# Squares of the last norm shared by ScalarE and VectorE, VectorE's tiles ahead of the last sums, another PSUM bank for v's first product, biases loaded earlier

## The chip, the cores and the metric

One core of one Trainium2 chip runs the whole kernel. The metric is the device time of one execution in microseconds (us); lower is better. The engines are TensorE (PE, with its weight load PEld), VectorE (DVE), ScalarE (ACT), GpSimd (POOL) and SyncE (SP), which here only issues transfers. All of them work in order, each from its own stream, and meet through semaphores.

## The reference

A decoder layer over 1024 tokens of width 1024, all float32, and a last RMSNorm:

```python
h = rmsnorm(x, norm1_g)
q, k, v, u = split(h @ w_in)                    # 4 x 512 columns
attn = diff_attention(q, k, v, ...)             # 4 heads, causal, two softmaxes each
pool = multiscale_pool(u, ...)                  # trailing means, windows 2, 4, 8, 16
x = x + concat(attn, pool) @ w_out
h = rmsnorm(x, norm2_g)
# top 4 of 32 experts; each expert, on its rows:
gate = minimum(xb @ w_gate[e] + b_gate[e], 7)
up   = clip(xb @ w_up[e] + b_up[e], -7, 7)
y    = (gate * sigmoid(1.702 * gate) * (up + 1)) @ w_down[e] + b_down[e]
x = x + sum over a token's experts of its gate value * y
out = rmsnorm(x, final_g)                       # x / sqrt(mean(x*x) + eps) * g
```

## The kernel before, in words

Tokens lie on the 128 partitions in 8 tiles of 128 rows (TB = 8), or transposed with features on the partitions. The work goes through five stages.

1. Input norm and projections. A list `jobs` sets the order of PE's products; each job is one PSUM bank of 512 columns that DVE or ACT empties. `bank_of(n)` gives the bank: n modulo 8 for the jobs up to `first_late` (34 jobs, so the last k product, job 33, sits in bank 1), and after them banks 1 and 3 in turn, beginning with v's first product (L294). A product waits until the bank's previous user has been emptied (`user_before`, `emptied`). After v's first product come the first attention scores, which wait until the first 34 jobs have been emptied.
2. Attention and pooling, 32 units of a token tile and a head, with the v and u products mixed in by hand (`slots_a`).
3. Output product, second norm and routing, tile by tile (b = 0 to 7). SP stores x1 and h2 of each tile to HBM (L399, L401). Before the last tile's stores it waits for the whole output product and loads the three bias tables of 32 rows (L397). PE turns them (`turn_bias`, L1677) behind the last logits, and ACT copies them out (L814). The tables lie in hT, ACT's square of the last tile goes to the scratch tile `junk_h`.
4. 32 experts, one after another. Each is six groups of 64 matmuls on 2 MB of weights that SP loads ahead; POOL gathers the tokens' rows and adds results back into HBM (`x_rows`).
5. The last norm, laid around the last group of products of expert 31. When the rows of the experts before it are in HBM, SP loads x1's eight tiles into `x2` (L439). POOL gathers expert 31's own rows (L622). ACT squares and sums each tile (`squares_of_rows`, L857). POOL multiplies tiles 0 to 3 by g (`tensor_tensor`, L640), each behind its tile's square. DVE waits for all eight sums (`squares_f`), computes 1/sqrt of the means in 12 small steps (`rsqrt_mean_dve`, L87 to L100) and signals `rstd_f`. Then ACT scales tiles 0 to 3 (L863), and DVE does tiles 4 to 7 in one step each (`normed_row`, L1363). SP writes the tiles out in the order 4, 1, 5, 2, 6, 3, 7 (L443, L446), POOL writes tile 0 (L643). DVE also adds the bias to the two halves of expert 31's last product: `down(0)` ahead of the wait for the sums, `down(1)` between its tiles 6 and 7 (both L1254 here). PE turns these halves back (L1873). `last_rows` adds them to the gathered rows (L1350), ACT squares (L873), DVE takes the second rsqrt and scales (L1359), and POOL scatters these rows over the output (L632). Before this scatter POOL waits until every one of the eight tiles has been written.

The order on DVE at the end of expert 31 is this:

```python
down(0)
f.n = 0
f.did(dve.memset(ss_l, 1.0))
dve.wait_ge(gf_in, 16)
dve.wait_ge(squares_f, TB)
rsqrt_mean_dve(dve, f, rstd[:, :], ss[:, :], tmp[:, :, :], D)
f.need()
dve.sem_inc(rstd_f, 1)
for b in range(SCALED, TB - 1):     # SCALED = 4
    normed_row(b)
down(1)
last_rows(nh)                       # begins with normed_row(TB - 1)
```

Of the kernel before, what the change touches and what calls it, by code (L numbers as in the profile page):

```python
# [12 lines left out]
P = 128  # L13
S, D = 1024, 1024
TB, KC = S // P, D // P
# [5 lines left out]
E, TOPK = 32, 4  # L21
# [13 lines left out]
SCALED = 4  # L35
# [67 lines left out]
def layer(nc, d, rows, out):  # L103
    with ExitStack() as ctx:
        sb = lambda name, shape, dt=F32: ctx.enter_context(nc.sbuf_tensor(name, shape, dt))
        sem = lambda name: ctx.enter_context(nc.semaphore(name))
        ps = ctx.enter_context(nc.psum_tensor("ps", [P, 8, HALF], F32))


        x = sb("x", [P, TB, D])  # L110
        xn = sb("xn", [P, TB, D])
        hT = sb("hT", [P, KC, S])
# [8 lines left out]
        ident = sb("ident", [P, P])  # L121
# [6 lines left out]
        bias = early[:, :].rearrange("p (i m e) -> p i m e", i=3, e=E)  # L128
# [4 lines left out]
        lam = sb("lam", [P, 8])  # L133
        ss, rstd, tmp = sb("ss", [P, TB]), sb("rstd", [P, TB]), sb("tmp", [P, 3, TB])
# [24 lines left out]
        x1T = xn[:, 1].rearrange("p (k t) -> p k t", t=P)  # L159
        h2 = [hT[:, 6], hT[:, 7], xn[:, 2], xn[:, 3]]  # L160

        junk_h, ss_h = xn[:, 4], lam[:, 6:7]
        late = xn[:, 6:8].rearrange("p a n -> p (a n)")
        r = Routes()
        r.slot = late[:, 0:256].rearrange("p (b e) -> p b e", e=E)
# [17 lines left out]
        flat = hT[:, :, :].rearrange("p k n -> p (k n)")  # L183
        taken = [0]

        def of_hT(*shape, dt=F32):

            n = math.prod(shape)
            words = n if dt in (F32, I32) else n // 2
            a = flat[:, taken[0]:taken[0] + words]  # L190
            taken[0] += words
            assert taken[0] <= KC * S
            names = "abc"[:len(shape)]
            a = a if dt == F32 else a.bitcast(dt)
            if len(shape) == 1:
                return a
            return a.rearrange(f"p ({' '.join(names)}) -> p {' '.join(names)}", **{c: s for c, s in zip(names, shape)})

        xg = of_hT(2, D)
        xT, aT = of_hT(KC, SLOTS), of_hT(KC, SLOTS)  # L200

        bias_rows = flat[0:E, 2 * D:2 * D + 3 * D].rearrange("p (i n) -> p i n", i=3)
        gt, ut, sg = (of_hT(4, SLOTS) for _ in range(3))
        tok = of_hT(TB, 6, dt=BF16)
        tab = [of_hT(4, dt=I32) for _ in range(3)]
# [16 lines left out]

        x2 = qk[:, :, :, :].rearrange("p a (b c) n -> p (a b) (c n)", c=2)

        junk_f, x_last = x[:, 7], xg
        small_f = x[:, 4, MORE * E:MORE * E + 10]
        ss_l, rstd_l, tmp_l = small_f[:, 0:2], small_f[:, 2:4], small_f[:, 4:10].rearrange("p (i h) -> p i h", h=2)

        x_in = [sem(f"x_in{b}") for b in range(TB)]
        vec_in, lam_ld, g2_in, wp_in, rw_in, rb_in = (sem(n) for n in ("vec_in", "lam_ld", "g2_in", "wp_in", "rw_in", "rb_in"))  # L230
        w_in, w_q_in = [sem(f"w_in{i}") for i in range(6)], sem("w_q_in")
        biases_in = sem("biases_in")
# [11 lines left out]
        out_mm, x1_ready, h2_ready, sq2 = (sem(n) for n in ("out_mm", "x1_ready", "h2_ready", "sq2"))  # L244
# [22 lines left out]
        squares_f, ready_f, ready_a, rstd_f, times_g = (sem(n) for n in ("squares_f", "ready_f", "ready_a", "rstd_f", "times_g"))  # L267
# [8 lines left out]
        first_late = len(jobs)  # L276
# [13 lines left out]
        def bank_of(n):  # L290

            if n == len(jobs) - 1:
                return 6
            return n % 8 if n < first_late else (1, 3)[(n - first_late) % 2]  # L294

        def user_before(n):

            return next((m for m in range(n - 1, -1, -1) if bank_of(m) == bank_of(n)), None)
# [46 lines left out]
        with nc.Block() as block:  # L345

            @block.sync
            def _(sp):
# [42 lines left out]
                sp.wait_ge(o_done, TB)  # L391
                sp.dma_start(w[2], weights(0, 2)).then_inc(w_ready[2], 16)
                for b in range(TB):
                    if b == TB - 1:
                        sp.wait_ge(out_mm, 2 * TB)
                        for i, bias in enumerate((d["b_gate"], d["b_up"], d["b_down"])):
                            sp.dma_start(bias_rows[:, i, :], bias[0]).then_inc(biases_in, 16)  # L397
                    sp.wait_ge(x1_ready, 2 * (b + 1))
                    sp.dma_start(rows.x1[b * P:(b + 1) * P, :], x[:, b, :]).then_inc(x1_st[b], 16)  # L399
                    sp.wait_ge(h2_ready, b + 1)  # L400
                    sp.dma_start(rows.h2[b * P:(b + 1) * P, :], h2[b % 4]).then_inc(h2_st[b], 16)  # L401
# [10 lines left out]
                for e in range(E):  # L412
                    for g, (src, c) in enumerate(sources):
                        n = e * GROUPS + g
# [261 lines left out]
            def _(act):  # L676
# [173 lines left out]
                        turn_in(j + 1)  # L850

                def squares_of_rows(again):
                    for b in range(TB):
                        act.wait_ge(x_in[b], 32 + 16 * again)
                        if b or again:
                            act.wait_ge(squares_f, again * TB + b)
                        act.activation(junk_f, x2[:, b, :], ACT.Square, accum_out=ss[:, b:b + 1]).then_inc(squares_f, 1)  # L857

                squares_of_rows(0)
                act.wait_ge(rstd_f, 1)  # L860
                for b in range(SCALED):
                    act.wait_ge(times_g, b + 1)
                    act.activation(x2[:, b, :], x2[:, b, :], ACT.Copy, scale=rstd[:, b:b + 1]).then_inc(ready_a, 1)  # L863
                act.wait_ge(squares_f, TB)
                act.sem_inc(passed, 1)

                def squares_of_last(nh):
# [23 lines left out]
            def _(dve):  # L891
# [441 lines left out]
                f = Order(dve, order_f)  # L1333

                def last_rows(nh):

                    normed_row(TB - 1)
                    dve.wait_ge(last_in, 32)
                    last_tab = tab[(E - 1) % 3]
                    for h in range(nh):  # L1340
                        n = HALVES[h]
                        by = last_tab[0:n, 2 + h:3 + h].bitcast(F32)
                        if nh == 1:
                            dve.wait_ge(pair_free, PAIRS + E * GROUPS)
                            dve.scalar_tensor_tensor(y[:, 0, :], t_rows, by, x_last[:, 0, :], ALU.mult, ALU.add).then_inc(last_z, 1)
                        else:
                            dve.wait_ge(back_mm[h], E + 1)
                            halves = lambda a: a.rearrange("p (a n) -> p a n", a=2)
                            at = (side, 0)[h]
                            dve.scalar_tensor_tensor(halves(y[0:n, h, :]), ps[0:n, at:at + 2, :], by, halves(x_last[0:n, h, :]),  # L1350
                                                     ALU.mult, ALU.add).then_inc(last_z, 1)
                    dve.wait_ge(last_sq, nh)
                    g = Order(dve, order_f, f.n)
                    rsqrt_mean_dve(dve, g, rstd_l, ss_l, tmp_l, D)
                    g.need()
                    assert g.n == STEPS_L
                    for h in range(nh):
                        n = HALVES[h]
                        dve.scalar_tensor_tensor(x_last[0:n, h, :], y[0:n, h, :], rstd_l[0:n, h:h + 1], g2[0:n, :], ALU.mult,  # L1359
                                                 ALU.mult).then_inc(last_f, 1)  # L1360

                def normed_row(b):
                    dve.scalar_tensor_tensor(x2[:, b, :], x2[:, b, :], rstd[:, b:b + 1], g2[:, :], ALU.mult, ALU.mult).then_inc(ready_f, 1)  # L1363
# [3 lines left out]
                def item(nh):  # L1367
                    n = (P, SLOTS)[nh - 1]
                    down = (lambda c: rows_down(E - 1, c)) if nh == 1 else (lambda c: down_in(E - 1, n, c))
                    for c in range(2):  # L1370
                        gate_in(E - 1, n, c)
                        up_in(E - 1, n, c)
                    down(0)
                    f.n = 0
                    f.did(dve.memset(ss_l, 1.0))
                    dve.wait_ge(gf_in, 16)
                    dve.wait_ge(squares_f, TB)
                    rsqrt_mean_dve(dve, f, rstd[:, :], ss[:, :], tmp[:, :, :], D)
                    f.need()
                    dve.sem_inc(rstd_f, 1)  # L1380
                    for b in range(SCALED, TB - 1):
                        normed_row(b)
                    down(1)
                    last_rows(nh)
                past_first(dve, wide, item)

                def all_rows():
                    dve.wait_ge(squares_f, 2 * TB)
                    g = Order(dve, order_f, f.n + STEPS_L)
                    rsqrt_mean_dve(dve, g, rstd[:, :], ss[:, :], tmp[:, :, :], D)  # L1390
                    g.need()
                    for b in range(TB):
                        normed_row(b)
# [41 lines left out]
            def _(pe):  # L1435
# [42 lines left out]
                for t in range(TB // 2):  # L1478
                    pe.wait_ge(x_in[t], 16)
                    for k in range(KC - 1):  # L1480
                        ins = pe.transpose(ps[:, bank_of(k), t * P:(t + 1) * P], x[:, t, k * P:(k + 1) * P], ident[:, :])
# [192 lines left out]
                def turn_bias(i, at):  # L1674
                    pe.wait_ge(biases_in, 48)
                    for m in range(KC):
                        ins = pe.transpose(ps[:, at, m * E:(m + 1) * E], bias_rows[:, i, m * P:(m + 1) * P], ident[0:E, 0:E])  # L1677
                    ins.then_inc(bias_mm, 1)

                turn_bias(0, 4)  # L1680
# [186 lines left out]
                with pe.If(width_of(pe, E - 1) > 0):  # L1867
                    pe.wait_ge(y_ready, 2 * E)
                    for c in range(2):
                        pe.wait_ge(pair_free, E * GROUPS + PAIRS - 1 + c)  # L1870
                        for h, n in enumerate(HALVES):
                            for k in range(4 * c, 4 * c + 4):
                                ins = pe.transpose(ps[0:n, (side, 0)[h] + c, (k - 4 * c) * P:(k - 4 * c + 1) * P],  # L1873
                                                   yT[:, k, h * P:h * P + n], ident[:, :])
# [35 lines left out]
def build(nc, d, out):  # L1910
    layer(nc, d, Rows(nc), out)
# [21 lines left out]
```

## Time and profile before

| | us |
|---|---|
| median of 3 runs (2072.66 to 2073.78) | 2072.96 |
| the profiled execution, its own time | 2074.92 |
| its span, first to last instruction | 2073.2 |
| PE busy | 2011.8 (97% of the span) |
| DVE, ACT, POOL busy | 655.5, 283.8, 232.9 |

The mean granted TensorE clock was 0.99 of full speed. The rows further down are of the profiled execution; their times count from its first instruction. A row of the timeline gives start, duration, engine, line and operation, and in brackets how long the engine had been idle before it and what released it. Rows whose engine ends in q (SPq) are the issue of a transfer, not its movement.

### The profile page before, as it was taken

Reading aid. Unit: us, or ns where it says so; the run is one execution under the profiler, and the core shown is the slowest. Engines: PE = TensorE matmul, PEld = TensorE weight load, DVE = VectorE, ACT = ScalarE, POOL = GpSimd, SP = SyncE. Lnnn points to the kernel's source line nnn. Section 1 sums busy time; section 2 is a strip of 40 time slices with the busy share of each in tenths; the row PEclk is TensorE's granted clock in tenths of the full one; section 3 lists DMA queues with packets and bytes.
Section 4 is the critical chain, followed back from the end, with each engine's and each line's share of the span. In section 5 each row is a group of like instructions: output and inputs, shape, how many; then the busy total and the mean of one; then the engine's idle time right before and its main releaser. Section 6 shows DMA issues by size and latency. Waiting matters only on the chain.

```text
span 2073.2 us, 32125 instructions
## 1 busy us (share of the span) xinstructions
PE 2011.8 (97%) x13457; PEld 1643.8 (79%) x13458; DVE 655.5 (32%) x1363; ACT 283.8 (14%) x457; POOL 232.9 (11%) x381
## 2 busy tenths in 40 slices
PE   8999988996999999999999999999999999999996
PEld 4444455554998898889788999988888888989996
DVE  3115676443223222222222332222222222222223
ACT  2001245111011001101001010111010100100103
POOL 0001333212000001000001010010000000000103
PEclk9999999997999999999999999999999999999998
DMA  4210022214878879998999988899899998887855
GB/s 173 81 41 1 1 92 84 100 61 152 305 248 305 307 272 322 321 329 296 321 322 318 309 294 272 286 319 335 312 304 322 319 319 310 279 299 260 287 189 199
DMA packets 231449, 500.89 MB, mean 242 GB/s; under 512 B 7766, under 2 KB 8303, under 8 KB 231298
## 3 DMA queue, kind: packets, MB, share of 16 engines
q1 hardware_dynamic: 218880, 454.46, 61.0%
q0 software_dynamic: 12368, 44.26, 8.6%
q8 instruction: 113, 1.85, 0.4%
q14 instruction: 38, 0.31, 0.0%
q10 hardware_dynamic: 50, 0.01, 0.0%
HBM read 463.63 MB, written 35.13 MB: 241 GB/s over the span
## 4 chain that ended last, share of the span: by engine, by line
PE 72%; DMA 1%; DVE 1%; issue 1%; SPq 0%; ACT 0%; POOL 0%; POOLq 0%; DVEq 0%; ACTq 0%
PE ps L1694 57%; PE ps L1721 12%; PE ps L1708 2%; PE ps L1714 1%; PE ps L1701 1%; DMA qk<-x_rows 1%; DMA out<-qk 0%; DVE x L1254 0%; DMA hT<-h_rows,hT 0%; DMA x_rows<-x,hT 0%; DVE qk L1363 0%; SPq L439 0%; DVE xn L1221 0%; ACT hT L821 0%; ACT x L857 0%
## 5 line engine op out<-in xcount | busy, mean ns | idle before, releaser
L1694 PE MATMUL ps<-hT,qk 128*128 128x128 f32 (+8 forms) x4096 | 501.7, 284 | 6.8 <-issue 6.8
L1694 PEld LDWEIGHTS ps<-hT,qk 128*128 128x128 f32 x4096 | 493.5, 192 | 16.6 <-issue 16.0
L1721 PE MATMUL ps<-w_ring,hT 128*128 128x512 f32 x576 | 251.8, 593 | 0.0
L1694 PE MATMUL ps<-hT,u_all 128*128 128x128 f32 (+8 forms) x2048 | 247.7, 282 | 0.0
L1694 PE MATMUL ps<-hT,v 128*128 128x128 f32 (+8 forms) x2048 | 247.7, 282 | 0.0
L1694 PEld LDWEIGHTS ps<-hT,v 128*128 128x128 f32 x2048 | 244.6, 191 | 0.0
L1694 PEld LDWEIGHTS ps<-hT,u_all 128*128 128x128 f32 x2048 | 244.6, 191 | 0.0
L1694 PE MATMUL ps<-hT,w_ring 128*128 128x132 f32 (+7 forms) x1792 | 233.8, 291 | 5.0 <-DVE x L1254 3.6
L1694 PEld LDWEIGHTS ps<-hT,w_ring 128*128 128x128 f32 x1792 | 229.3, 190 | 7.4 <-issue 7.0
L1721 PEld LDWEIGHTS ps<-w_ring,hT 128*128 128x128 f32 x576 | 107.5, 190 | 126.7 <-issue 126.3
L558 POOL DMA_INDIRECT hT<-h_rows,hT x46 | 45.3, 986 | 1148.9 <-issue 672.1
L825 ACT ACTIVATE hT<-hT 128x768 f32<-128x768 f32 x64 | 53.9, 842 | 855.5 <-DVE hT L1235 855.5
L1467 PE MATMUL ps<-hT,w_ring 128*128 128x512 f32 x384 | 168.9, 595 | 1.3 <-DMA w_ring<-in_w_in 1.3
L1467 PEld LDWEIGHTS ps<-hT,w_ring 128*128 128x128 f32 x384 | 71.5, 190 | 86.7 <-issue 83.7
L1241 DVE TENSOR_TENSOR hT<-ps,early 128x512 f32<-128x512 f32 (+1 forms) x64 | 51.7, 808 | 241.3 <-PE ps L1694 234.0
L1232 DVE TENSOR_TENSOR hT<-ps,early 128x512 f32<-128x512 f32 (+1 forms) x64 | 51.7, 808 | 212.9 <-PE ps L1694 191.1
L563 POOL DMA_INDIRECT x_rows<-x,hT x44 | 70.1, 1593 | 266.9 <-ACT x L836 220.1
L821 ACT COPY hT<-ps 128x1024 f32<-128x1024 f32 x64 | 51.2, 800 | 338.8 <-PE ps L1708 298.5
L1262 DVE TENSOR_TENSOR x<-ps,x 128x512 f32<-128x512 f32 x36 | 24.9, 692 | 220.4 <-PE ps L1721 220.4
L1254 DVE TENSOR_TENSOR x<-ps,early 128x768 f32<-128x768 f32 x28 | 26.8, 958 | 193.5 <-PE ps L1694 193.5
L1239 DVE TENSOR_TENSOR hT<-hT 128x512 f32<-128x512 f32 (+1 forms) x64 | 52.4, 818 | 65.8 <-ACT hT L825 65.8
L1203 DVE COPY hT<-ps 128x12 f32<-128x12 f32 x31 | 5.3, 171 | 180.5 <-PE ps L1701 180.5
(250 smaller groups left out, 1470.6 us busy)
## 6 DMA issues: line engine op xcount, KB each, us to landing
w_ring<-in_w_down SPq DMA_DIRECT2D x64, 2048.0 KB, 7.9
qk<-in_w_gate SPq DMA_DIRECT2D x32, 2048.0 KB
qk<-in_w_up SPq DMA_DIRECT2D x32, 2048.0 KB
v<-in_w_gate SPq DMA_DIRECT2D x32, 2048.0 KB, 10.5
u_all<-in_w_up SPq DMA_DIRECT2D x32, 2048.0 KB, 8.7
x<-in_b_down SPq DMA_DIRECT2D x32, 512.0 KB, 11.6
w_ring<-in_w_in SPq DMA_DIRECT2D x3, 2048.0 KB, 9.0
x<-in_x SPq DMA_DIRECT2D x8, 512.0 KB, 12.4
```

The costliest lines, as they stand in the source:

```text
L558: return pool.indirect_dma_start(out=xg[0:n, h, :], out_offset=None, in_=rows.h2[:, :], in_offset=bass.IndirectOffsetOnAxis(ap=tab_e[0:n, ...
L563: return pool.indirect_dma_start(out=rows.x1[:, :], out_offset=bass.IndirectOffsetOnAxis(ap=tab_e[0:n, h:h + 1].bitcast(U32), axis=0), in_ ...
L821: act.copy(xT[:, :, h * P:h * P + n], turned_in[h]).then_inc(xT_ready, 1)
L825: act.activation(sg[:, :, :], gt[:, :, :], ACT.Sigmoid, scale=ALPHA).then_inc(sg_ready, 1)
L1232: dve.tensor_tensor(gt[:, :, 0:n], pair[2 * c % PAIRS][:, :, 0:n], bcast(r.bias[:, 0, 4 * c:4 * c + 4, e], n), ALU.add).then_inc(pair_free, 1)
L1239: dve.tensor_tensor(sg[:, :, 0:n], gt[:, :, 0:n], sg[:, :, 0:n], ALU.mult).then_inc(gate_s, 1)
L1241: dve.tensor_tensor(ut[:, :, 0:n], pair[(2 * c + 1) % PAIRS][:, :, 0:n], bcast(r.bias[:, 1, 4 * c:4 * c + 4, e], n), ALU.add).then_inc(pai ...
L1254: dve.tensor_tensor(yT[:, 4 * c:4 * c + 4, 0:n], pair[(4 + c) % PAIRS][:, :, 0:n], bcast(r.bias[:, 2, 4 * c:4 * c + 4, e], n), ALU.add).th ...
L1467: ins = pe.matmul(bank, ring[:, tile_of[what] % 2, k, a * P:(a + 1) * P], hT[:, k, b * HALF:(b + 1) * HALF], start=k == 0, stop=k == KC - 1)
L1694: ins = pe.matmul(bank[:, m, 0:n], w[g][:, k, m * P:(m + 1) * P], rhs[:, k, 0:n], start=k == 0, stop=k == KC - 1)
L1708: ins = pe.transpose(turned_in[h][:, k, :], xg[0:n, h, k * P:(k + 1) * P], ident[0:n, 0:n])
L1721: ins = pe.matmul(ps[:, 2 * (g % PAIRS), :], aT[:, k, 0:P], w[g][:, k, :], start=k == 0, stop=k == KC - 1)
```

## The change

- `bank_of`: the late jobs take banks 3 and 1 in turn, so that v's first product goes to bank 3. The last user of that bank is job 27.
- The biases are loaded at b = 5 of SP's loop, with no wait for the output product. They go to other places (`xn[0:E, 5]`, `hT[0:E, 4]`, `xn[0:E, 4]`), and `junk_h` moves from `xn[:, 4]` to `xn[:, 0]`.
- ACT squares tiles 0 to 3 of the last norm alone. DVE squares tiles 4 to 7 with `tensor_tensor_reduce`, the instruction that it uses for squares of the first norm (L897), into another scratch tile. Its wait on `squares_f` is for four.
- `down(0)` moves from ahead of the squares to behind the rsqrt; tile 7 moves ahead of `down(1)`, so that DVE's four tiles follow one another.

```diff
-            return n % 8 if n < first_late else (1, 3)[(n - first_late) % 2]
+            return n % 8 if n < first_late else (3, 1)[(n - first_late) % 2]
...
-                    if b == TB - 1:
-                        sp.wait_ge(out_mm, 2 * TB)
+                    if b == TB // 2 + 1:
                         for i, bias in enumerate((d["b_gate"], d["b_up"], d["b_down"])):
-                            sp.dma_start(bias_rows[:, i, :], bias[0]).then_inc(biases_in, 16)
+                            sp.dma_start(bias_rows[i], bias[0]).then_inc(biases_in, 16)
...
-                    for b in range(TB):
+                    for b in range(TB if again else TB // 2):
                         act.wait_ge(x_in[b], 32 + 16 * again)
...
                         act.activation(junk_f, x2[:, b, :], ACT.Square, accum_out=ss[:, b:b + 1]).then_inc(squares_f, 1)
...
-                    normed_row(TB - 1)
                     dve.wait_ge(last_in, 32)
...
-                    down(0)
                     f.n = 0
                     f.did(dve.memset(ss_l, 1.0))
+                    for b in range(TB // 2, TB):
+                        dve.wait_ge(x_in[b], 32)
+                        f.need()
+                        f.did(dve.tensor_tensor_reduce(junk_v, x2[:, b, :], x2[:, b, :], 1.0, 0.0, ALU.mult, ALU.add,
+                                                       accum_out=ss[:, b:b + 1]))
                     dve.wait_ge(gf_in, 16)
-                    dve.wait_ge(squares_f, TB)
+                    dve.wait_ge(squares_f, TB // 2)
                     rsqrt_mean_dve(dve, f, rstd[:, :], ss[:, :], tmp[:, :, :], D)
                     f.need()
                     dve.sem_inc(rstd_f, 1)
-                    for b in range(SCALED, TB - 1):
+                    down(0)
+                    for b in range(SCALED, TB):
                         normed_row(b)
                     down(1)
                     last_rows(nh)
```

## Rows read from the trace of the kernel before

**Rows 1.** The page's chain that ended last: shares of the span by line.

```profile
PE ps L1694 57%; PE ps L1721 12%; PE ps L1708 2%; PE ps L1714 1%; PE ps L1701 1%; DMA qk<-x_rows 1%; DMA out<-qk 0%; DVE x L1254 0%; DMA hT<-h_rows,hT 0%; DMA x_rows<-x,hT 0%; DVE qk L1363 0%; SPq L439 0%; DVE xn L1221 0%; ACT hT L821 0%; ACT x L857 0%
```

**Rows 2.** Busy time by stretch: PE, PEld, DVE, ACT, POOL; PEclk, DMA share, GB/s.

```profile
522.00:1990.00 1468.00, 1462.11 (x11147) 1316.71 (x11146) 400.05 (x720) 149.32 (x167) 110.37 (x86) 1.00 0.88 303
...
2053.00:2054.00 1.00, 1.00 (x9) 1.00 (x8) 1.00 (x2) 1.00 (x2) 0.59 (x1) 1.00 0.44 180
2054.00:2064.00 10.00, 2.51 (x20) 1.98 (x18) 8.35 (x18) 3.94 (x6) 0.81 (x1) 0.78 1.02 396
```

**Rows 3.** Timeline at v's first product.

```profile
127.61 7.11 PE L1461 MATMUL ps<-w_ring,hT 128*128 128x512 f32 x16 [0.88 <-DVE qk L934]
```

**Rows 4.** Timeline between the output product and the first expert.

```profile
487.87 0.34 SPq L397 DMA_DIRECT2D hT<-in_b_gate  x1
...
491.42 1.18 PE L1677 MATMUL ps<-ident,hT 32*128 32x32 f32 x16 [0.39 <-DMA hT<-in_b_down]
...
492.64 0.34 SPq L401 DMA_DIRECT2D h_rows<-xn  x1
...
493.50 0.21 PE L1630 MATMUL ps<-member,tri 128*128 128x32 bf16 x1 [0.90 <-DVE member L1118]
```

**Rows 5.** Timeline of the last norm.

```profile
2039.25 9.31 POOL L640 TENSOR_TENSOR qk<-qk,g 128x1024 f32<-128x1024 f32 x4
...
2041.12 1.06 ACT L857 ACTIVATE x<-qk 128x1024 f32<-128x1024 f32 x1
...
2043.20 1.06 ACT L857 ACTIVATE x<-qk 128x1024 f32<-128x1024 f32 x1 [0.93 <-DMA qk<-x_rows]
...
2046.54 1.06 ACT L857 ACTIVATE x<-qk 128x1024 f32<-128x1024 f32 x1 [2.19 <-DMA qk<-x_rows]
...
2047.78 1.06 ACT L857 ACTIVATE x<-qk 128x1024 f32<-128x1024 f32 x1
...
2049.02 0.17 DVE L87 TENSOR_SCALAR tmp<-ss 128x8 f32<-128x8 f32 x1 [3.20 <-ACT x L857]
...
2051.37 4.27 ACT L863 ACTIVATE qk<-qk,rstd 128x1024 f32<-128x1024 f32 x4 [2.44 <-DVEq L1380]
2051.44 3.68 DVE L1363 SCALAR_TENSOR_TENSOR qk<-qk,rstd,g 128x1024 f32<-128x1024 f32 x3 [0.16 <-DVE rstd L100]
2052.75 0.34 SPq L446 DMA_DIRECT2D out<-qk  x1
...
2055.03 0.95 DVE L1254 TENSOR_TENSOR x<-ps,early 128x768 f32<-128x768 f32 x1
...
2055.21 1.94 PE L1873 MATMUL ps<-ident,x 128*128 128x128 f32 x16 [0.64 <-issue]
...
2057.09 2.46 DVE L1350 SCALAR_TENSOR_TENSOR x<-ps,hT 128x1024 f32<-128x1024 f32 x2
...
2063.06 2.47 DVE L1359 SCALAR_TENSOR_TENSOR hT<-x,g 128x1024 f32<-128x1024 f32 x2
2067.62 0.99 POOL L632 DMA_INDIRECT out<-hT  x1 [12.80 <-issue]
```

**Rows 6.** The chain in order of time, the last wait ahead of POOL's scatters.

```profile
2058.76 7.57 DMA out<-qk
```

**Rows 7.** Timeline in the attention stage where POOL and DVE instructions meet.

```profile
176.70 1.03 POOL L502 TENSOR_TENSOR xn<-xn 128x512 f32<-128x512 f32 x1 [116.30 <-DVE xn L1029]
...
176.90 0.85 DVE L1015 SCALAR_TENSOR_TENSOR soft<-soft,lam 128x1 f32<-128x1 f32 x1
...
214.71 1.22 DVE L983 TENSOR_TENSOR v<-u_all 128x1023 f32<-128x1023 f32 x1
...
214.87 1.95 POOL L502 TENSOR_TENSOR xn<-xn 128x512 f32<-128x512 f32 x1 [27.15 <-DVE xn L1029]
...
216.02 1.88 DVE L983 TENSOR_TENSOR v<-v 128x1022 f32<-128x1022 f32 x1
```

**Rows 8.** All squares of the first norm on DVE: shortest, median and longest, ns.

```profile
L897 DVE CUSTOM_DVE_ANT_0 u_all<-x x4: 1225/1226/1227, 5.9 to 20.0; 128x1024 f32<-128x1024 f32 x4
```

More of the change, by code:

```diff
@@ L160, in layer @@
         h2 = [hT[:, 6], hT[:, 7], xn[:, 2], xn[:, 3]]
-        junk_h, ss_h = xn[:, 4], lam[:, 6:7]
+        junk_h, ss_h = xn[:, 0], lam[:, 6:7]
         late = xn[:, 6:8].rearrange("p a n -> p (a n)")
@@ L200, in layer @@
         xT, aT = of_hT(KC, SLOTS), of_hT(KC, SLOTS)
-        bias_rows = flat[0:E, 2 * D:2 * D + 3 * D].rearrange("p (i n) -> p i n", i=3)
+        bias_rows = [xn[0:E, 5], hT[0:E, 4], xn[0:E, 4]]
         gt, ut, sg = (of_hT(4, SLOTS) for _ in range(3))
@@ L223, in layer @@
         x2 = qk[:, :, :, :].rearrange("p a (b c) n -> p (a b) (c n)", c=2)
-        junk_f, x_last = x[:, 7], xg
+        junk_f, junk_v, x_last = x[:, 7], xn[:, 3], xg
         small_f = x[:, 4, MORE * E:MORE * E + 10]
@@ L852, in squares_of_rows @@
                 def squares_of_rows(again):
-                    for b in range(TB):
+                    for b in range(TB if again else TB // 2):
                         act.wait_ge(x_in[b], 32 + 16 * again)
                         if b or again:
-                            act.wait_ge(squares_f, again * TB + b)
+                            act.wait_ge(squares_f, again * (TB // 2) + b)
                         act.activation(junk_f, x2[:, b, :], ACT.Square, accum_out=ss[:, b:b + 1]).then_inc(squares_f, 1)
@@ L863, in _ @@
                     act.activation(x2[:, b, :], x2[:, b, :], ACT.Copy, scale=rstd[:, b:b + 1]).then_inc(ready_a, 1)
-                act.wait_ge(squares_f, TB)
+                act.wait_ge(squares_f, TB // 2)
                 act.sem_inc(passed, 1)
@@ L1387, in all_rows @@
                 def all_rows():
-                    dve.wait_ge(squares_f, 2 * TB)
+                    dve.wait_ge(squares_f, TB // 2 + TB)
                     g = Order(dve, order_f, f.n + STEPS_L)
@@ L1676, in turn_bias @@
                     for m in range(KC):
-                        ins = pe.transpose(ps[:, at, m * E:(m + 1) * E], bias_rows[:, i, m * P:(m + 1) * P], ident[0:E, 0:E])
+                        ins = pe.transpose(ps[:, at, m * E:(m + 1) * E], bias_rows[i][:, m * P:(m + 1) * P], ident[0:E, 0:E])
                     ins.then_inc(bias_mm, 1)
```

## The prediction

> **What bounds the kernel now.** I read the chain that ended last first. By line it is PE's products of the experts, the matmuls of L1694 and L1721 [rows 1]; the view by stretch says the same, since from 522 to 1990 us PE works 1462.1 of 1468 us at a granted clock of 1.00 [rows 2]. The change takes no work from PE. So only two kinds of place can move the time: a gap in PE's stream ahead of the experts, which moves everything after it, and the stretch behind the last products, where PE no longer matters.
>
> Second I read the timeline at the edges. There is one gap that the change touches, 0.88 us ahead of v's first product, released by a DVE eviction [rows 3].
>
> Third, the end. In the last norm ACT squares tile 6 at 2046.54, when it lands, and tile 7 at 2047.78; DVE's rsqrt starts at 2049.02, its first tile at 2051.44, the first output write is issued at 2052.75 [rows 5]. From then on the transfers are the limit: 180 GB/s in the microsecond from 2053, 396 GB/s at a share of 1.02 over the next ten [rows 2]. The last write is issued at 2058.76 and lands 7.57 us later, at 2066.33 [rows 6]; POOL's first scatter goes at 2067.62 [rows 5], and the span ends at 2073.2, 6.9 us after the landing. So the end follows the moment at which output writes begin, not the moment at which the last tile is ready. The other strand, the last expert's own rows, is ready at 2063.06 + 2.47 = 2065.53 and waits for the writes [rows 5].
>
> **Bank of v's first product.** In bank 1 it waits for the eviction of the last k product. In bank 3 the previous user is six jobs older, so the wait is gone. v's first product takes 7.11 us of PE [rows 3], far more than the eviction, so the scores behind it, which want that eviction too, find it done. What follows hangs on PE or on waits counted from it, the transfers of later weights included, so the gain is passed on whole: -0.88 us. Its bounds are 0, if another wait takes it up further on, and -0.88.
>
> **Biases.** Three loads leave SP's queue at 487.87 and go to an idle moment at b = 5. PE waited 0.39 us for them at 491.42, but behind the two turns it waits again, 0.90 us, for DVE's `member` at 493.50 [rows 4]. What comes earlier in PE only lengthens that second wait. The x1 store of tile 7 gets up to 1.3 us earlier, yet h2's store, which the gather needs as well, waits for the norm and stays at 492.64 [rows 4]. At b = 5 SP has nothing queued. Cost 0; without the second wait it would be a gain of 0.39.
>
> **Squares on two engines.** Counted without anything in between, nothing is won: the last sum is not late for want of an engine but because tile 6 lands at 2046.54. DVE has both late tiles, 6 and 7, one after the other, and one square takes it 1.226 us [rows 8]. From 2046.54 that is 2046.54 + 2 x 1.23 = 2049.0, and the rsqrt starts at 2049.02 today.
>
> Something is in between, though. POOL multiplies tiles 0 to 3 from 2039.25 for 9.31 us, 2.33 each [rows 5], and today DVE has nearly nothing to do then. In the attention stage the two meet. POOL's 128x512 multiply takes 1.03 us alone; begun 0.16 us behind a DVE tensor_tensor it takes 1.95, until 216.82. The next DVE one begins at 216.02 and takes 1.88 in place of 1.22: it ends 1.08 us after POOL's end. Even a 128x1 instruction begun 0.20 us after POOL's start takes 0.85 and ends 0.02 after it [rows 7]. So they take turns by whole instructions: one of DVE with two inputs in SBUF does not run beside one of POOL. The squares read `x2` twice and are of that kind. No row shows a square itself against POOL, so the bounds are no hold at all and a hold for every one.
>
> The Trainium skill (GPSIMD Engine Reference, Specifications) says that GpSimd's SBUF interfaces are shared with VectorE, with contention from VectorE instructions that have two SBUF inputs; it gives no price. By it the squares are held and the time is the 2076.9 below; by the row of the squares alone, which ran with POOL idle, it would be 2073.0.
>
> I take the hold. Tile 4 is there by about 2041.1 (ACT took it at 2041.12 with no wait), inside POOL's first multiply, 2039.25 to 2041.58. Then they alternate: square 4 to 2042.66, multiply 1 to 2044.96, square 5 (landed 2043.2) to 2046.04, multiply 2 to 2048.35, square 6 to 2049.43, multiply 3 to 2051.75, square 7 to 2052.8. As a sum: 2039.25 + 9.31 + 4 x 1.08 = 2052.88. The rsqrt starts some 0.05 later, at 2052.9, not at 2049.02: **+3.9 us**. If every turn costs a full 1.23 it is +4.5. POOL's multiplies end 3.2 us later, at 2051.75. ACT needs the fourth three scalings of 1.07 after its start, which itself moves to 2055.3 [rows 5], so that costs nothing.
>
> **down(0) behind the rsqrt.** It takes 0.95 us, as the same instruction at 2055.03 [rows 5], and now stands between rstd and DVE's first tile. SP's order begins with that tile, and the write of tile 1 is behind it in SP's queue. So the first write moves by another **+0.9** to 2052.75 + 3.9 + 0.9 = 2057.6. The first half was hidden in DVE's wait for the squares; that cover is gone. Tile 1's write then follows at once (0.84 us behind today's first), which may give back 0.1; I keep +0.9 within 0.5 to 1.0.
>
> **Tile 7 ahead of down(1).** The four tiles at 1.23 end at about 2061.2 and down(1) at 2062.2, against 2055.98 today: +6.2. Its followers are PE's turns, L1350, ACT's squares, the second rsqrt and L1359. If PE's part keeps its 1.1 us, L1359 starts at 2069.3; PE has been idle long by then, and at the half clock that the mean of 0.78 contains [rows 2] it is 2.2 us and 2070.4. Its two results come at 2071.6 and 2072.9. The writes land at 2066.33 + 4.8 = 2071.1, POOL wants the first result about half a microsecond later, and the second 1.3 us after the first. It fits, with hardly anything to spare. Cost 0.
>
> **Sum.** -0.88 + 0 + 3.9 + 0.9 = +3.9 us. On the profiled execution that is 2074.92 + 3.9 = 2078.8 (span 2077.1). This execution lies 1.96 above the median of the runs, so the median is 2072.96 + 3.9 = **2076.9**.
>
> **The rivals.**
> - No hold: the squares do not share what the multiplies need. For it: they are another instruction than those in rows 7. Against it: they read two streams from SBUF at 1.226 us, as the tensor_tensor with its 1.22 does. Then +0.9 for down(0) against -0.88: 2073.0.
> - The last rows become the gate, the slower side. PE's turns behind down(1) run at half clock and, with the first half's eight delayed into them, take 3.9 us (twice 1.94) in place of 1.1. L1359 then starts at 2072.1, its first result comes at 2073.3, POOL waits 1.7 us for it: 2078.6. It decides from about 0.1 us of delay beyond what I count.
> - The gap ahead of v only moves: something else in the attention stage takes the 0.88 us. PE is busy there with gaps of its own, which speaks a little for it. 2077.8.
> - Fewer turns: the last tiles' landings are set by one slow stretch of the load (2.19 us of waiting for tile 6), and if tile 4 came before POOL starts, square 7 would stand ahead of the last multiply. That takes 2.3 off: 2074.6.
>
> **How the numbers follow.** Turns with the writes as gate: 0.60, own range 2076.0 to 2077.8. No hold 0.13, last rows 0.12, gap moved 0.08, fewer turns 0.07. For this kernel 0.2%, 4.1 us, is about what a measurement can tell from no change, so slower begins at 2077.1. Above it lie the last rows (0.12), most of the moved gap (0.07) and a third of the likeliest case (0.21), that is 0.40. Faster would need 4.1 us, and nothing here has more than 0.9: 0.01. Same: 0.59. The range takes in no hold below and the last rows above: 2072.6 to 2078.8.
>
> **What the profile after would show.** v's first product with no idle time ahead. DVE rows of squares among the tail's rows, of some 1.5 to 3 us in place of 1.23, and POOL's four multiplies 3 us longer in total. L87 some 3.9 us later against the last landing, then L1254 ahead of four tiles, and the first output write 4.8 later. PE's turns of the biases without a wait, but the one for `member` longer. I am wrong if the squares show 1.23 us each beside POOL, or if POOL's scatter is released by L1359 and not by the last write.

## The result, and the profile after

The changed kernel takes 2078.07 us (median of 12 runs, 2076.20 to 2079.71), the kernel before, timed beside it, 2073.62 (12 runs, 2072.06 to 2074.74). The ratio is 1.0024, with a 95% interval of 1.0016 to 1.0031: 4.45 us slower, where +3.9 was forecast. The time lies in the stated range of 2072.6 to 2078.8, and 1.17 us above the forecast of 2076.9. 0.66 of that is the kernel before, whose median was 2072.96 when I forecast and is 2073.62 here; the other 0.5 is the change itself. It is also 0.3 above the range of the likeliest case (2076.0 to 2077.8). With 0.24% it is just beyond the 0.2% that separates slower from no change in the prediction, the side to which I had given 0.40, and "same" 0.59.

The timeline of the last norm in the changed kernel, the counterpart of [rows 5]:

```profile
2034.48 17.32 PE L1698 MATMUL ps<-hT,w_ring 128*128 128x180 f32 x112 [0.36 <-DVE hT L1247]
...
2036.46 9.28 POOL L639 TENSOR_TENSOR qk<-qk,g 128x1024 f32<-128x1024 f32 x4
...
2038.22 8.62 DVE L1377 CUSTOM_DVE_ANT_0 xn<-qk 128x1024 f32<-128x1024 f32 x1 [3.88 <-DMA qk<-x_rows]
...
2046.99 1.22 DVE L1377 CUSTOM_DVE_ANT_0 xn<-qk 128x1024 f32<-128x1024 f32 x1
...
2048.36 1.23 DVE L1377 CUSTOM_DVE_ANT_0 xn<-qk 128x1024 f32<-128x1024 f32 x1
...
2049.74 1.22 DVE L1377 CUSTOM_DVE_ANT_0 xn<-qk 128x1024 f32<-128x1024 f32 x1
...
2051.11 0.17 DVE L87 TENSOR_SCALAR tmp<-ss 128x8 f32<-128x8 f32 x1
...
2053.58 0.96 DVE L1254 TENSOR_TENSOR x<-ps,early 128x768 f32<-128x768 f32 x1 [0.21 <-DVE rstd L100]
2054.45 4.86 DVE L1362 SCALAR_TENSOR_TENSOR qk<-qk,rstd,g 128x1024 f32<-128x1024 f32 x4
...
2055.76 0.34 SPq L445 DMA_DIRECT2D out<-qk  x1
...
2060.24 1.97 PE L1877 MATMUL ps<-ident,x 128*128 128x128 f32 x8 [4.49 <-DVE x L1254]
...
2067.44 2.47 DVE L1358 SCALAR_TENSOR_TENSOR hT<-x,g 128x1024 f32<-128x1024 f32 x2
2070.74 0.99 POOL L631 DMA_INDIRECT out<-hT  x1 [14.12 <-DVE hT L1358]
```

POOL begins its multiplies at 2036.46 and ends them at 2045.74, as fast as before. DVE's square of tile 4 is released by its landing at 2038.22 and lasts 8.62 us, until 2046.84, which is 1.10 us behind POOL's end. The other three then take 1.22 or 1.23 each. The rsqrt starts 14.65 us after POOL's first multiply (2051.11 - 2036.46), where it was 9.77 in [rows 5] (2049.02 - 2039.25). Then comes down(0), 0.96 us, and then the first tile.

Two executions don't reach this stretch at the same moment, so I measure from the start of PE's last 112 matmuls. In the kernel before these start at 2037.26:

```profile
2037.26 17.32 PE L1694 MATMUL ps<-hT,w_ring 128*128 128x180 f32 x112 [0.36 <-DVE hT L1247]
```

There the first output write comes 15.49 us after it (2052.75) and the end 35.94 (2073.2); in the changed kernel 21.28 (2055.76 - 2034.48) and 41.82 (2076.3 - 2034.48). The tail is 5.9 us longer, and 5.8 of it is there when the writes begin.

The chain in order of time says that the writes are still what the end waits for, as in [rows 6]. It runs to the landing of the last write, 2061.29 + 8.16 = 2069.45:

```profile
2038.22 8.62 DVE xn L1377
...
2061.29 8.16 DMA out<-qk
```

The timeline puts L1358 as the releaser beside POOL's scatter (2070.74), the sign by which the prediction would have been wrong. It isn't so: L1358's first result, the only one that the first scatter needs, was there at about 2068.7. The scatter starts 1.29 us after the landing, and before it was 1.29 as well (2066.33 to 2067.62).

The view by stretch, the counterpart of [rows 2], shows the writes at nearly the same rate, 401 GB/s where it was 396. PE turns the second half of the last expert's rows at a granted clock of 0.50, which is its level of 1.2 GHz, after 4.49 us without work:

```profile
2057.00:2067.00 10.00, 1.97 (x8) 1.41 (x8) 7.17 (x15) 3.02 (x5) 0.00 (x0) 0.50 1.02 401
```

At v's first product, the counterpart of [rows 3], the idle time is gone:

```profile
125.58 7.03 PE L1465 MATMUL ps<-w_ring,hT 128*128 128x512 f32 x16
```

It starts 2.03 us earlier than in the execution of before. 0.88 of that is the gap; the other 1.15 is a difference between the two executions ahead of this place. By the start of the last 112 matmuls the lead is 2.78 us, and so these two spans differ by only 3.1 us (5.9 - 2.8). The medians differ by 4.45: over many executions the lead is smaller, 1.4 us if the tail is 5.9 us longer in all of them. 0.88 of that is the gap, the rest is not explained.

Around the biases, the counterpart of [rows 4]:

```profile
442.36 0.89 SPq L396 DMA_DIRECT2D xn<-in_b_gate  x1
...
490.47 0.32 SPq L400 DMA_DIRECT2D h_rows<-xn  x1
```

```profile
488.80 0.68 PE L1681 MATMUL ps<-ident,xn 32*128 32x32 f32 x8
489.32 1.01 PE L1681 MATMUL ps<-ident,hT 32*128 32x32 f32 x8
491.33 0.21 PE L1634 MATMUL ps<-member,tri 128*128 128x32 bf16 x1 [1.00 <-DVE member L1118]
```

The turns have no wait ahead of them any more. They take 1.53 us from first start to end (490.33 - 488.80) where they took 1.18, and the wait for `member` has grown from 0.90 to 1.00 us.

### The profile page after: what moved, and what is told of

Read it like the earlier page. It is cut to its first block, busy times and chain, and to the rows that moved or that the text cites. A ratio compares the mean times of both kernels' runs of the same rounds, so it can differ in the third digit from the quotient of the medians.

```text
span 2076.3 us, 32125 instructions
## 1 busy us (share of the span) xinstructions
PE 2012.2 (97%) x13457; PEld 1644.4 (79%) x13458; DVE 667.5 (32%) x1371; ACT 278.9 (13%) x449; POOL 232.2 (11%) x381
## 4 chain that ended last, share of the span: by engine, by line
PE 72%; DVE 1%; DMA 1%; issue 1%; SPq 0%; ACT 0%; POOL 0%; POOLq 0%; DVEq 0%
PE ps L1698 57%; PE ps L1725 12%; PE ps L1712 2%; PE ps L1718 1%; PE ps L1705 1%; DVE xn L1377 1%; DMA out<-qk 0%; DMA qk<-x_rows 0%; DVE x L1254 0%; DMA hT<-h_rows,hT 0%; DVE qk L1362 0%; DMA x_rows<-x,hT 0%; DVE xn L1221 0%; SPq L438 0%; ACT hT L820 0%
```

## The experiments

The tail is always the time from the start of PE's last 112 matmuls to the end of the span, in the profiled execution. Each tail is a single one. The kernel before, v_and_biases and v_bank_alone have the same last norm and show 35.9, 35.5 and 35.4 us, so I read nothing into differences of half a microsecond.

| kernel | median us (runs) | before beside it | ratio (95%) | first write, us into the tail | tail us |
|---|---|---|---|---|---|
| before | | | | 15.49 | 35.9 |
| changed | 2078.07 (12) | 2073.62 | 1.0024 (1.0016 to 1.0031) | 21.28 | 41.8 |
| squares_on_act | 2073.49 (11) | 2073.29 | 0.9999 (0.9990 to 1.0008) | 16.57 | 37.1 |
| down0_first | 2077.14 (11) | 2073.29 | 1.0018 (1.0009 to 1.0027) | 20.39 | 41.0 |
| v_and_biases | 2072.10 (11) | 2073.29 | 0.9995 (0.9986 to 1.0004) | 15.15 | 35.5 |
| pool_waits_own | 2077.15 (10) | 2073.29 | 1.0019 (1.0009 to 1.0028) | 20.11 | 40.7 |
| gather_late | 2070.11 (11) | 2072.90 | 0.9986 (0.9977 to 0.9995) | 13.42 | 33.9 |
| v_bank_alone | 2072.32 (11) | 2072.90 | 0.9997 (0.9988 to 1.0006) | 15.04 | 35.4 |
| no_multiplies | 2072.86 (1) | 2072.90 | | 15.93 | 36.7 |
| plain_product | 2077.15 (1) | 2072.90 | | 21.11 | 41.7 |

**squares_on_act: the squares back on ACT, the new order kept.**

```diff
-                    for b in range(TB if again else TB // 2):
+                    for b in range(TB):
...
-                    for b in range(TB // 2, TB):
-                        dve.wait_ge(x_in[b], 32)
-                        f.need()
-                        f.did(dve.tensor_tensor_reduce(...))
...
-                    dve.wait_ge(squares_f, TB // 2)
+                    dve.wait_ge(squares_f, TB)
```

> The changed kernel with all eight squares back on ACT; down(0) stays behind the rsqrt and tile 7 ahead of down(1). Measure of the tail: from the start of PE's last 112 matmuls to the end of the span, 35.9 us before and 41.8 us in the changed kernel. If DVE's squares beside POOL's multiplies are what costs most (theory), the tail is 36.9 us, the 0.95 us of down(0) above before, and the whole time is that of before within 0.5 us (0.9 gained at v, 0.95 lost here). If instead the order of down(0), the tiles and down(1) is what costs (rival: the last rows become the gate), the tail stays above 39 us and the time at 2 us or more over before.

The tail is 37.1 us and the time that of before. The timeline:

```profile
2044.59 1.06 ACT L857 ACTIVATE x<-qk 128x1024 f32<-128x1024 f32 x1
2048.18 4.27 ACT L863 ACTIVATE qk<-qk,rstd 128x1024 f32<-128x1024 f32 x4 [2.44 <-DVEq L1378]
2048.30 0.96 DVE L1254 TENSOR_TENSOR x<-ps,early 128x768 f32<-128x768 f32 x1 [0.21 <-DVE rstd L100]
...
2050.48 0.34 SPq L445 DMA_DIRECT2D out<-qk  x1
```

ACT's own square of tile 7 starts at 2044.59, and it is scaling tile 0 3.59 us later, as in [rows 5] (2051.37 - 2047.78). The squares on DVE cost 41.8 - 37.1 = 4.7 us by the tails. The medians against the kernel before beside each give 4.3 (4.45 - 0.20). The new order alone costs 37.1 - 35.9 = 1.2, in which down(0) is 0.96. The late down(1) shows only as the small rest, if at all.

**down0_first: down(0) ahead of the squares.**

```diff
+                    down(0)
                     f.n = 0
                     f.did(dve.memset(ss_l, 1.0))
...
                     dve.sem_inc(rstd_f, 1)
-                    down(0)
```

> The changed kernel with down(0) back ahead of the squares, where DVE waits anyway for POOL's multiplies to end. Theory: POOL's four multiplies run to their end whatever DVE does, the squares follow, so down(0) is hidden: first output write 0.9 us earlier against the start of PE's last matmuls, tail 40.9 us in place of 41.8, time about 3.6 us over before in place of 4.5. Rival (DVE's squares would be let in between if they came at other moments): tile 4's square starts only after down(0), so the order of the two engines changes and the tail moves by more than 1.5 us either way.

```profile
2035.51 9.31 POOL L639 TENSOR_TENSOR qk<-qk,g 128x1024 f32<-128x1024 f32 x4
...
2041.11 0.96 DVE L1254 TENSOR_TENSOR x<-ps,early 128x768 f32<-128x768 f32 x1 [7.74 <-PE ps L1698]
...
2042.23 3.67 DVE L1378 CUSTOM_DVE_ANT_0 xn<-qk 128x1024 f32<-128x1024 f32 x1 [0.16 <-DVE x L1374]
```

down(0), one of whose inputs is in PSUM, runs in 0.96 us beside POOL. The square, begun at 2042.23, waits again for POOL's end at 2044.82 and is done at 2045.90, 1.08 behind it. So asking 1.8 us or 6.7 us after POOL's start makes no difference to when the squares are done. The first write comes 0.9 us earlier and the tail is 0.8 shorter. The chain in order of time goes through the last rows here, in place of a write's landing:

```profile
2066.78 1.28 DVE hT L1358
...
2068.97 0.45 POOL out L631
```

That can't be what released the scatter. It is the second result of L1358, done at 2068.06, and the first scatter (`wait_ge(last_f, h + 1)`, h = 0) needs only the first, which was there at about 2066.8. The last output write, asked for by itself:

```profile
L445 SPq DMA_DIRECT2D out<-qk x1: 1248/1248/1248, 2059.4 to 2059.4; - x1
...
DMA to landing us min/median/max: 8.3/8.3/8.3
```

It lands at about 2067.7 (2059.38 + 8.3), and the scatter starts 1.3 us later, the same distance as in the kernel before and in the changed kernel. So the writes are the gate here too; the second result only happened to come at a step of POOL's way to its scatter.

**pool_waits_own: each multiply of POOL waits for the one before it.**

```diff
                         pool.wait_ge(squares_f, b + 1)
+                        if b:
+                            pool.wait_ge(times_g, b)
                         pool.tensor_tensor(x2[:, b, :], x2[:, b, :], g2[:, :], ALU.mult).then_inc(times_g, 1)
```

> The changed kernel with one added wait: each of POOL's four multiplies waits for the one before it to be finished. Theory (POOL keeps what both engines need as long as its next multiply is ready to go, and DVE gets in when POOL has to wait for its own result): DVE's squares come in between, tile 4's square takes some 1.5 to 3.5 us in place of 8.6, POOL's four multiplies stretch from 9.3 to 12 us or more, and DVE's rsqrt starts 13.6 us after POOL's first multiply, where it is 14.65 in the changed kernel: time about 1 us less. Rival (this kind of DVE instruction always loses against POOL): tile 4's square again lasts until POOL's last multiply ends, and nothing moves.

```profile
2038.39 2.37 POOL L641 TENSOR_TENSOR qk<-qk,g 128x1024 f32<-128x1024 f32 x1
...
2040.46 1.39 DVE L1379 CUSTOM_DVE_ANT_0 xn<-qk 128x1024 f32<-128x1024 f32 x1 [4.20 <-DMA qk<-x_rows]
2040.91 9.73 POOL L641 TENSOR_TENSOR qk<-qk,g 128x1024 f32<-128x1024 f32 x3
2042.87 2.27 DVE L1379 CUSTOM_DVE_ANT_0 xn<-qk 128x1024 f32<-128x1024 f32 x1 [1.01 <-DMA qk<-x_rows]
...
2046.00 2.43 DVE L1379 CUSTOM_DVE_ANT_0 xn<-qk 128x1024 f32<-128x1024 f32 x1 [0.85 <-DMA qk<-x_rows]
...
2048.58 3.14 DVE L1379 CUSTOM_DVE_ANT_0 xn<-qk 128x1024 f32<-128x1024 f32 x1
...
2051.86 0.17 DVE L87 TENSOR_SCALAR tmp<-ss 128x8 f32<-128x8 f32 x1
```

This is the picture of the prediction. The engines take turns; POOL's four multiplies last from 2038.39 to 2050.64, 12.3 us; the rsqrt starts 13.47 us after the first of them, where the prediction had 13.65 (2052.9 - 2039.25) and the changed kernel 14.65. A wait that seems idle makes the tail 1.1 us shorter; the medians (+3.9 us here, +4.45 in the changed kernel) agree in direction, but their intervals overlap. In these two kernels what decides is whether POOL has its next instruction ready.

**plain_product: DVE without the sum.** The sums of tiles 4 to 7 are left out.

```diff
-                        f.did(dve.tensor_tensor_reduce(junk_v, x2[:, b, :], x2[:, b, :], 1.0, 0.0, ALU.mult, ALU.add,
-                                                       accum_out=ss[:, b:b + 1]))
+                        f.did(dve.tensor_tensor(junk_v, x2[:, b, :], x2[:, b, :], ALU.mult))
```

> The changed kernel with a plain tensor_tensor product in place of the square with a sum on DVE (the sums of tiles 4 to 7 are left out). Theory (what matters is POOL's run of multiplies without a wait between them): tile 4's product also lasts until POOL's last multiply ends, some 8.6 us. Rival (the instruction with a sum is the one that cannot get in): tile 4's product takes under 4 us and POOL's multiplies are stretched beyond 9.3 us.

The four products of DVE by line, shortest, median and longest in ns:

```profile
L1377 DVE TENSOR_TENSOR xn<-qk x4: 1224/1225/8360, 2037.7 to 2048.9; 128x1024 f32<-128x1024 f32 x4
```

The longest takes 8.36 us: a plain tensor_tensor, of the kind that took turns with POOL in [rows 7], is shut out as well. So it is not a matter of the instruction with a sum.

**no_multiplies: POOL's four multiplies taken out.** Tiles 0 to 3 go out without the factor g.

```diff
-                        pool.tensor_tensor(x2[:, b, :], x2[:, b, :], g2[:, :], ALU.mult).then_inc(times_g, 1)
+                        pool.sem_inc(times_g, 1)
```

> The changed kernel without POOL's four multiplies by g (tiles 0 to 3 go out without the factor; the signal to ACT is kept). Theory: with POOL out of the way DVE squares each tile when it lands, 1.23 us each, and its rsqrt starts about 2.5 to 3.0 us after tile 6's landing, as ACT's did, not 7.8 us as in the changed kernel; tail of about 37 us in place of 41.8. Rival (the square on DVE is slow by itself in this place, or held by the transfers into x2): tile 4's square stays at several us.

```profile
2037.94 1.23 DVE L1377 CUSTOM_DVE_ANT_0 xn<-qk 128x1024 f32<-128x1024 f32 x1 [3.71 <-DMA qk<-x_rows]
...
2042.61 1.22 DVE L1377 CUSTOM_DVE_ANT_0 xn<-qk 128x1024 f32<-128x1024 f32 x1 [1.87 <-DMA qk<-x_rows]
...
2044.27 1.22 DVE L1377 CUSTOM_DVE_ANT_0 xn<-qk 128x1024 f32<-128x1024 f32 x1 [0.42 <-DMA qk<-x_rows]
...
2045.64 0.17 DVE L87 TENSOR_SCALAR tmp<-ss 128x8 f32<-128x8 f32 x1
```

With POOL quiet each square takes its 1.23 us when its tile lands, and the tail is 36.7 us. Yet the last square starts when tile 7 lands, and the rsqrt 1.37 us after that; ACT had 1.24 in [rows 5]. With the load as it is, shared squares win nothing even without the collision.

**v_and_biases and v_bank_alone: the last norm untouched.** The first is the kernel before with the new bank and the early biases (their parts of the diff, nothing else), the second with the new bank alone.

> The kernel before with the other bank for v's first product and the early biases, the last norm untouched. Theory: 0.9 us faster than before, all of it from the bank; no idle time ahead of L1461's first matmul (0.88 before) and the tail 35.9 us. Rival (the gap only moves): same time as before, and PE idle 0.88 us more elsewhere between v's first product and the experts.

> The kernel before with v's first product in bank 3 and nothing else. Theory: 0.9 us faster than before and the same as with the biases too (the biases are worth nothing). Rival (the early biases carry part of it): within 0.3 us of before, and slower than v_and_biases.

The idle time ahead of v's first product is gone in both. The medians lie 1.2 and 0.6 us below before, but both intervals hold 1, and the two kernels can't be told from each other. A gain of 0.9 us fits both, no gain is not excluded by the times, and how the 0.9 splits on the bank and the biases they don't say. For that I have only the profile.

The rival in which the gap only moves would make the stretch from v's first product to the start of the last 112 matmuls 0.88 us longer: 1909.65 us in the kernel before (2037.26 - 127.61), so 1910.5. In the nine profiled executions with the new bank it is 1907.1 to 1910.0 us (v_bank_alone: 2033.92 - 126.03 = 1907.89). That speaks against the rival. It does not settle it, as these nine differ by 3 us and there is one execution of before.

**gather_late: a version that beats both.** v_and_biases with one move: POOL gathers the last expert's rows behind its multiplies.

```diff
-                past_first(pool, wide[E - 1], rows_of_last)
...
                         pool.tensor_tensor(x2[:, b, :], x2[:, b, :], g2[:, :], ALU.mult).then_inc(times_g, 1)
+                    past_first(pool, wide[E - 1], rows_of_last)
```

> The kernel before with the other bank, the early biases and one more move: POOL gathers the last expert's own rows behind its four multiplies in place of ahead of them. The last norm's order is that of the kernel before, with all squares on ACT. Theory: x1's eight tiles are loaded without the gather's 0.77 MB beside them and the last tile lands 2 to 3 us earlier against the load's issue (16.2 us from the first issue to the start of tile 7's square before), DVE's rsqrt and the first output write follow, so the time is 2 to 3 us below v_and_biases. Rival: the slow pieces of the load are not the gather's doing, and the last square starts when it did: same time as v_and_biases within 0.5 us.

```profile
2029.41 5.08 SPq L438 DMA_DIRECT2D qk<-x_rows  x8
...
2035.57 9.33 POOL L638 TENSOR_TENSOR qk<-qk,g 128x1024 f32<-128x1024 f32 x4 [9.66 <-ACT x L856]
...
2043.21 1.06 ACT L856 ACTIVATE x<-qk 128x1024 f32<-128x1024 f32 x1
...
2044.45 0.47 DVE L87 TENSOR_SCALAR tmp<-ss 128x8 f32<-128x8 f32 x1 [0.80 <-ACT x L856]
...
2048.51 0.34 SPq L445 DMA_DIRECT2D out<-qk  x1
```

The eight pieces of x1's load by their line:

```profile
L438 SPq DMA_DIRECT2D qk<-x_rows x8: 338/436/1570, 2029.4 to 2034.0; - x8
...
DMA to landing us min/median/max: 4.8/7.1/9.1
```

The slowest piece of the load lands 9.1 us after its issue, where it took 12.1 in v_and_biases. From the first issue of the load to the start of tile 7's square it is now 13.80 us; it was 16.46 in the profile of before and 16.12 in that of v_and_biases (2044.81 - 2028.69). That part moved by 2.3 us against v_and_biases, within what I expected. The time fell less than I said: 2.8 us below before where v_and_biases was 1.2 below, and a tail of 33.9 after 35.5, so 1.6 us and not 2 to 3. Two pieces of the rest are in the rows. L87, the rsqrt's first step, takes 0.47 us in place of 0.17, as POOL's last multiply runs until 2044.90; it reads only one tensor from SBUF and is held all the same. And the load is issued 0.25 us later against PE's last matmuls than in v_and_biases. The ratio to before is 0.9986 (0.9977 to 0.9995), a gain of 0.14% whose interval just leaves out 1.

Two things are different in this kernel and would decide what to try next; no run here tests them. ACT's eight squares follow each other with 0.17 us of idle time in all, so ACT and no longer the landing sets the start of tile 7's square. And the chain that ended last goes through PE's last products, down(1) and tile 7 behind it:

```profile
2035.09 17.33 PE ps L1693 x112
...
2052.45 0.96 DVE x L1253
2053.41 1.21 DVE qk L1362
...
2054.63 7.56 DMA out<-qk
```

The last write waits for tile 7 and not for SP's queue, which was free 0.69 us earlier (2052.68 + 1.26 = 2053.94).

## Why the prediction was right, and where its size was off

**What sets the end.** Right: the output writes. The first moves by 5.8 us and the end by 5.9, the rate of the writes is nearly the same, and so is the way from the last landing to POOL's scatter, 1.29 us.

**Bank of v's first product, -0.88.** The gap is gone, as forecast. That the gain reaches the end is consistent with the timings of v_and_biases and v_bank_alone, not shown by them.

**Biases, 0.** By the profile right, but the time won ahead of the turns is not all in the wait for `member`: that grew by 0.10, and the turns themselves take 0.35 longer. From PE's last eight matmuls for the logits to the first one on `member` it is 3.54 us (487.79 to 491.33), and it was 3.55 (489.95 to 493.50).

**Squares on two engines, +3.9.** That the two engines exclude each other was right; the order in which they do it was not, and so the size was off: 4.7 us by squares_on_act. The step that failed is "So they take turns by whole instructions" for POOL's four multiplies. In [rows 7] they do; but each POOL instruction there that follows another of its own waits for that one's result, and DVE gets in during that wait. The row behind those of [rows 7] shows it:

```profile
216.90 1.58 POOL L506 TENSOR_TENSOR xn<-xn 128x256 f32<-128x256 f32 x1
```

It starts 0.08 us after L502's end (216.82), and by then DVE's instruction, waiting since 216.02, has got in: DVE ends at 217.90, and this time it is POOL's that is held, at 1.58 us for half of the columns that took L502 1.03 alone. The four multiplies of the last norm wait only for ACT's squares, which are long done. POOL then went from one to the next with DVE shut out, for as long as 7.5 us (from 2038.22 to 2045.74). The order is not square, multiply, square, multiply but four multiplies, then four squares, one of them begun long before: 2045.74 + 1.10 + 3 x 1.38 + 0.13 = 2051.11, the start of L87. pool_waits_own brought the forecast order and its number back, no_multiplies took the cost away, and plain_product showed that it does not hang on the instruction with a sum. By the same count my own bound "a hold for every one" of +4.5 was too low too, and two of the signs that I named did not come: POOL's multiplies took no longer, and three of the squares took their normal time. That the number came so near owes something to luck: in either order POOL's 9.3 us and DVE's squares are laid end to end. The two sums differ by 1.0 us (14.65 against 13.65), nearly all of it in three squares, which cost 1.38 each from start to start when they follow one another, not 1.08.

The sentence of the Trainium skill (GPSIMD Engine Reference, Specifications) on contention with VectorE instructions of two SBUF inputs holds here: 8.62 us in place of 1.22. It doesn't say who wins and for how long, which was what mattered.

**down(0) behind the rsqrt, +0.9.** Right: 0.89 in the first write and 0.8 in the tail by down0_first.

**Tile 7 ahead of down(1), 0.** Right, and with more to spare than forecast. L1358's first result was there about 1.24 us after 2067.44, at 2068.7, 0.75 us ahead of the last write's landing at 2069.45; the forecast had it half a microsecond behind. Two terms were off and offset each other in part. down(1) came later than forecast by the squares' excess. What follows it was sized too large: PE's turns ran at half clock as feared (1.97 us for eight), but L1349 starts 1.27 us after down(1)'s end where it was 1.11 before, 0.16 more and not 1.1. Before, tile 7 stood between them on DVE (2055.90 + 1.28), so the 1.1 was not PE's.

**The sum.** -0.88 + 4.7 + 0.95 = +4.8 against +4.45 measured, in an interval of +3.3 to +6.4. With the right size of one term the forecast would have been on the slower side.

**The rivals.** No hold is refuted. The last rows as the gate did not happen, in down0_first neither. Fewer turns is refuted: all four of POOL's multiplies stood ahead of the last three squares. A gap at v that only moves is made unlikely by the profiles and is not excluded by the times.

## What to carry to other kernels

Before work goes from ScalarE to VectorE because VectorE is idle, look at what GpSimd does in that stretch: a VectorE instruction with two inputs in SBUF may have to wait for GpSimd's whole run of instructions, as here, where a 1.2 us square took 8.6. If the two must meet, a wait between GpSimd's instructions can help a little (1.1 us of 4.7 here); leaving the work where it was helped more. And ask first what the last input of the work is: here tile 7 landed too late for a second engine to help, and moving a transfer out of the load's way gained what sharing the squares could not. A releaser that a profile names is inferred: check that the instruction in the kernel really waits for it.

## What the runs showed of the hardware that I had not expected

- A run of GpSimd multiplies without a wait between them is not interrupted by VectorE: 9.28 us for four, a VectorE square of 1.22 us lasting 8.62 beside them, a plain product 8.36. With a wait for its own result ahead of each, GpSimd's four take 12.3 us and VectorE's squares 1.39 to 3.14 us.
- A VectorE add with one input in PSUM took 0.96 us in the midst of such a run, its normal time. But a tensor_scalar of 128x8 from SBUF to SBUF, which has one input tensor, took 0.47 us in place of 0.17 and ended 0.02 after POOL's last multiply (gather_late). So two inputs in SBUF are not needed for a hold; this is one row.
- Without POOL's gather of the last rows beside it, the slowest piece of x1's load landed 9.1 us after its issue and tile 7's square started 13.80 us after the first issue. With it these were 12.2 and 16.46 (before), 12.1 and 16.12 (v_and_biases).
